# A decoder's gated delta mixer: rows of decay and beta reach all partitions by GpSimd DMAs out of a DRAM scratch, where matmuls with a constant and ScalarE copies did it

## What is computed

```python
qkv, z, a, b = split(h @ w_in)
qkv = silu(causal_conv(qkv))                     # q, k, v of 8 heads
q, k = l2norm(q) * 128 ** -0.5, l2norm(k)
beta = sigmoid(b)                                # (time, 8 heads)
g = -exp(A_log) * softplus(a + dt_bias)          # (time, 8 heads)
G = cumsum(g within a chunk)
S_t = exp(g_t) (I - beta_t k_t k_t^T) S_{t-1} + beta_t k_t v_t^T;   o_t = S_t^T q_t
```

## Time and profile before

| | |
|---|---|
| time, median of 3 runs | 1976.42 us (1971.94 to 1976.88) |
| the profiled execution's own time | 1976.46 us |
| its span, first to last instruction | 1974.7 us |
| busy: PE, PEld, DVE, ACT, POOL | 92%, 87%, 57%, 33%, 0% |
| mean granted TensorE clock | 0.937 of full speed |
| DMA packets | 136.00 MB, mean 69 GB/s |

### The profile page before, as it was taken

One profiled execution on the slowest core, in us unless ns is written; L12 is line 12 of the kernel. 1 busy time (PEld: TensorE's weight loads), 2 busy tenths in 40 slices (PEclk: granted clock), 3 DMA queues, 4 the chain that ended last, 5 costly groups with the idle time before them and its releaser, 6 DMA issues. The chain is left out here.

```text
span 1974.7 us, 33936 instructions
## 1 busy us (share of the span) xinstructions
PE 1811.3 (92%) x13227; PEld 1714.2 (87%) x13227; DVE 1134.3 (57%) x2027; ACT 661.5 (33%) x1108; POOL 0.4 (0%) x5
## 2 busy tenths in 40 slices
PE   3899899998999999997799999999988999999997
PEld 3888888887999989997688888888867999999996
DVE  5777878785534334354666677667732643434344
ACT  1434444432212222222444455445522221222222
POOL 0000000000000000000000000000000000000000
PEclk9988989898999999998799999999957999999997
DMA  5122222222333323222112211211110333322321
GB/s 174 46 64 65 67 63 66 64 66 67 86 94 88 86 76 86 77 77 54 45 44 57 58 37 50 56 56 33 56 34 22 88 89 90 90 86 85 88 82 45
DMA packets 257436, 136.00 MB, mean 69 GB/s; under 512 B 6698, under 2 KB 255876, under 8 KB 257348
## 3 DMA queue, kind: packets, MB, share of 16 engines
q1 hardware_dynamic: 219700, 114.03, 20.4%
q10 hardware_dynamic: 37648, 20.68, 3.5%
HBM read 122.70 MB, written 12.00 MB: 68 GB/s over the span
## 5 line engine op out<-in xcount | busy, mean ns | idle before, releaser
L425 PE MATMUL pj<-xh,w_hi 128*128 128x272 f32 x2064 | 467.2, 309 | 29.8 <-DVE w_lo L1304 15.0
L425 PE MATMUL pj<-xl,w_hi 128*128 128x272 f32 x2064 | 440.4, 296 | 0.0
L425 PE MATMUL pj<-xh,w_lo 128*128 128x272 f32 x2064 | 439.4, 295 | 0.0
L865 ACT ACTIVATE w_hi<-w_raw 128x1024 fp32r<-128x1024 f32 x209 | 220.8, 1056 | 642.3 <-PE pj L425 623.9
L425 PEld LDWEIGHTS pj<-xh,w_hi 128*128 128x128 f32 x2064 | 335.6, 196 | 54.3 <-issue 26.8
L425 PEld LDWEIGHTS pj<-xl,w_hi 128*128 128x128 f32 x2064 | 338.5, 197 | 0.0
L425 PEld LDWEIGHTS pj<-xh,w_lo 128*128 128x128 f32 x2064 | 336.8, 197 | 0.0
L1304 DVE TENSOR_TENSOR w_lo<-w_raw,w_hi 128x1024 fp32r<-128x1024 f32 x209 | 254.8, 1219 | 45.9 <-ACT w_hi L865 45.7
L425 PE MATMUL pj<-oh,w_hi 128*128 128x272 f32 x1280 | 269.0, 292 | 12.7 <-DVE ol L1347 5.4
L425 PE MATMUL pj<-oh,w_lo 128*128 128x272 f32 x1280 | 266.0, 289 | 0.0
L425 PE MATMUL pj<-ol,w_hi 128*128 128x272 f32 x1280 | 266.0, 289 | 0.0
(11 more groups left out here) (275 smaller groups left out, 2050.8 us busy)
## 6 DMA issues: line engine op xcount, KB each, us to landing
w_raw<-in_mlp_w_up_dram SPq DMA_DIRECT2D x64, 512.0 KB, 3.9
w_raw<-in_mlp_w_down_dram SPq DMA_DIRECT2D x64, 512.0 KB, 3.7
w_raw<-in_hgrn_w_in_dram SPq DMA_DIRECT2D x32, 512.0 KB, 4.0
w_raw<-in_gdn_w_in_dram SPq DMA_DIRECT2D x32, 512.0 KB, 4.1
out_dram<-S ACTq DMA_DIRECT2D x16, 512.0 KB, 3.5
S<-in_state_hgrn_dram ACTq DMA_DIRECT2D x8, 512.0 KB, 4.0
w_raw<-in_hgrn_w_out_dram SPq DMA_DIRECT2D x8, 512.0 KB, 3.6
S<-in_state_gdn_dram ACTq DMA_DIRECT2D x8, 512.0 KB, 4.0
```

The source lines that it names most:

```text
L425: last = mm(pj[:, s, b, 0:HALF], w[:, s, k, :], v[:, k, b * HALF:(b + 1) * HALF], start=(k == 0 and a == 0), stop=(k == KT - 1 and a == 2))
L865: f(w_hi[:, c % SPLIT], w_raw[:, slot], ACT.Copy).then_inc(w_high, 1)
```

## The change

The constants for the indicator products and the head's column leave the constant tile, which shrinks from 1264 to 1000 columns. VectorE's select, PE's two products per head, ScalarE's two copies and its exp are gone, with the waits that guarded their PSUM banks. POOL waits for step `eg`, stores the three groups of eight rows of `gt4` into a DRAM tensor (3, 8, 544), waits for all three stores, and then loads for every head one row of each group onto 128 partitions: G as soon as step `qn` of the head before is done, beta and eG as soon as step `cols2` of the head before is done. VectorE waits for the loads at the three places where the tiles are read.

```diff
+            s = st["gp"][1]
+            pool.wait_ge(s.sem, s.after("eg", 0))
+            for n, r in enumerate((0, 32, 96)):
+                pool.dma_start(gates[n], gt4[r:r + H]).then_inc(gates_kept, 16)
+            pool.wait_ge(gates_kept, 48)
+            v = st["ga"][0]
+            for h in range(H):
+                if h:
+                    pool.wait_ge(v.sem, v.after("qn", h - 1))
+                pool.dma_start(gd["G"], gates[0, h].partition_broadcast(P)).then_inc(g_in, 16)
+                if h:
+                    pool.wait_ge(v.sem, v.after("cols2", h - 1))
+                pool.dma_start(gd["beta"], gates[1, h].partition_broadcast(P)).then_inc(beta_in, 16)
+                pool.dma_start(gd["eG"], gates[2, h].partition_broadcast(P)).then_inc(eg_in, 16)
...
-                if slot in ("L3", "L4"):
-                    g, name = (0, "gb") if slot == "L3" else (1, "bb")
-                    pe.wait_ge(s.sem, s.after("G" if g else "hist", h))
-                    pe.wait_ge(v.sem, v.after("gsel", h))
-                    for b in range(2):
-                        last = mm(rr[:, 2 + b, 0:HALF], cf[:, C_IND + g * P:C_IND + (g + 1) * P],
-                                  work[:, b * HALF:(b + 1) * HALF], start=True, stop=True)
-                    t.did(last, name)
...
-                        held((v, "sr3", h), *([] if nxt is None else [(sa, "G", nxt)]))
+                        held((v, "sr3", h))
...
-                        held((s, "rs", h), *([] if nxt is None else [(sa, "bb", nxt)]))
+                        held((s, "rs", h))
...
-                    sem_of(t, "gb", h)
-                    s.did(f(halves(G), rr[:, 2:4, 0:HALF], ACT.Copy), "G")
...
-                    sem_of(t, "bb", h)
-                    s.did(f(halves(gd["beta"]), rr[:, 2:4, 0:HALF], ACT.Copy), "bb")
...
-                    s.did(f(gd["eG"], G, ACT.Exp), "eG")
...
-                    v.did(ts(work, gt4[:], hc[:, 4:5], None, ALU.mult), "gsel")
...
-                    after(s, "G", h)
+                    after(v, "cols", h)
+                    dve.wait_ge(g_in, h * 16 + 16)
...
+                    dve.wait_ge(beta_in, h * 16 + 16)
                     v.did(tt(work, nK, gd["beta"], ALU.mult), "kb")
...
+                    dve.wait_ge(eg_in, h * 16 + 16)
                     v.did(tt(gd["qe"], nQ, gd["eG"], ALU.mult), "qe")
```

More of the change, by code:

```diff
@@ L42 @@
 V_N = V_CONV
-C_EYE, C_INCL, C_NSTR, C_IND, C_RESET, C_SEQ, C_INCLS, C_NSTRS, C_HSEL = 0, 128, 256, 384, 640, 1184, 1192, 1224, 1256
-C_W = C_HSEL + H
+C_EYE, C_INCL, C_NSTR, C_RESET, C_SEQ, C_INCLS, C_NSTRS = 0, 128, 256, 384, 928, 936, 968
+C_W = C_NSTRS + TS
 CU_HALF = len(LEVELS) * (T // 2)
@@ L70, in shape_constants @@
     cf[:, C_NSTR:C_NSTR + P] = -(p[None, :] > p[:, None]).astype(np.float32)
-    cf[0:32, C_IND:C_IND + P] = 1
-    cf[32:64, C_IND + P:C_IND + 2 * P] = 1
     t = np.arange(T)
@@ L80, in shape_constants @@
     cf[:TS, C_NSTRS:C_NSTRS + TS] = -(same & (s[None, :] > s[:, None])).astype(np.float32)
-    cf[:, C_HSEL:C_HSEL + H] = p[:, None] % 32 == np.arange(H)[None, :]
     cu = np.zeros((P, 2, len(LEVELS), T // 2), np.float32)
@@ L235, in build @@
             gp=["x", "neg", "ls", "g", "g2", "scan", "dl"],
-            ga=["cols", "gsel", "k1", "k2", "k3", "kneg", "kls", "q1", "q2", "q3", "qneg", "dec", "ks", "qls",
+            ga=["cols", "k1", "k2", "k3", "kneg", "kls", "q1", "q2", "q3", "qneg", "dec", "ks", "qls",
                 "v1", "v2", "v3", "vneg", "kn", "kb", "qs", "kkd", "vls", "vs", "qn", "zneg", "qkd", "nl", "tt0", "tt1",
@@ L251, in build @@
             gp=["A", "exp", "ln", "be", "el", "eg", "cols"],
-            ga=["hist", "past", "ktap", "qtap", "vhist", "kexp", "kln", "G", "ksig", "qexp", "qln", "bb", "dec",
-                "sqk", "vtap", "qsig", "lnk", "rnk", "eG", "sqq", "vexp", "vln", "vsig", "lnq", "rnq", "zexp", "zln", "cout",
+            ga=["hist", "past", "ktap", "qtap", "vhist", "kexp", "kln", "ksig", "qexp", "qln", "dec",
+                "sqk", "vtap", "qsig", "lnk", "rnk", "sqq", "vexp", "vln", "vsig", "lnq", "rnq", "zexp", "zln", "cout",
                 "K", "tm0", "zsig"],
@@ L265, in build @@
             gp=["cols"],
-            ga=["cin", "gb", "bb", "ssk", "kk", "ssq", "qk", "stash", "t0"],
+            ga=["cin", "ssk", "kk", "ssq", "qk", "stash", "t0"],
             gr=["x2", "dt2", "tr2", "vT", "x4", "dt4", "tr4", "kT", "x8", "sks", "dt8", "tr8", "x16", "dt16", "tr16",
@@ L274, in build @@
         ones_set = sem("ones_set")
+        gates_kept = sem("gate_rows_kept")
+        g_in = sem("decay_rows_spread")
+        beta_in = sem("beta_rows_spread")
+        eg_in = sem("decay_factors_spread")
+        gates = nc.dram_tensor("gate_rows", (3, H, T), F32, kind="Internal").ap()
         st = {}
@@ L683, in gdn_rec @@
                         gdn_prepare("L1", nxt)
-                    if m == 32 and nxt is not None:
-                        held((s, "rs", h))
-                        gdn_prepare("L4", nxt)
                     if m == 64 and nxt is not None:
@@ L1076, in gdn_prepare @@
                     norm_scale(work, "lnk", "rnk", h)
-                    s.did(f(gd["eG"], G, ACT.Exp), "eG")
                 if slot == "L6x":
-                    sem_of(s, "eG", h)
                     sem_of(v, "qs", h)
@@ L1584, in gdn_prepare @@
                 if slot == "L1":
-                    cp(hc[:, 4:5], cf[:, ds(h + C_HSEL, 1)])
                     cp(hcw[:], cw[:].rearrange("p j (g x) -> p j g x", g=3)[:, :, :, ds(h, 1)]
@@ L1588, in gdn_prepare @@
                     v.did(cp(gnext[:], of_head(0).rearrange("p c o -> p (c o)")), "cols")
-                    after(v, "cols", h)
-                    v.did(ts(work, gt4[:], hc[:, 4:5], None, ALU.mult), "gsel")
                     low(h * 4, U_GIN + 3)
```

## The result

The changed kernel takes 1985.89 us (median of 7 runs, 1980.38 to 1990.41), the kernel before, run beside it, 1974.25 us (7 runs, 1970.39 to 1977.94). The ratio is 1.0058, with a 95% interval of 1.0041 to 1.0075: slower by 11.6 us, where 1972.4 and no measurable difference had been forecast, and the time lies above the range.

The account below looks back on a forecast made before the run. PE, busy 1811.3 of 1974.7 us, was taken to set the pace. 3.29 + 0.35 + 0.51 + 0.32 - 0.40 = 4.07 us off 1976.46 gave 1972.4 us, counted as the same; range 1963 to 1981.

Parts of the forecast that it names:

- The sum: Whole kernel: beta's product 3.29, G's product 0.35, head 0 0.51, constants 0.32, less waits 0.40, gives 4.07 us gained.
- the four rivals: Alternatives: all PE time returns (0.20), waits eat the gain (0.08), POOL's DMAs hold VectorE (0.10), clock falls (0.06).
- rival 4: Recurrences: PE's clock falls to half in more stretches; 1996 us with two more each, 1984 with one; chance 0.06.
- the mixer's terms: Second mixer: 3.29 for beta's product, 0.35 for G's, 0.51 for head 0, less 0.40 us for waits.
- G's product: In seven recurrences: removing it leaves PE waiting for Tt's copy, so only 0.05 us each, 0.35 us in all.
- beta's product: In seven recurrences: without it VectorE's merge (L1719) starts 0.47 us earlier, behind `w_lo`; 3.29 us in all.
- rival 1: All PE time of the 64 removed records, 15.4 us, comes back; 1960.7 us; chance 0.20.
- The start: Kernel start: the constant tile shrinks by 132 KB, so everything waiting for constants begins 0.32 us earlier.
- Head 0: Head 0's preparation, with no recurrence to hide it: 0.51 us of ScalarE's chain go.
- The loads: GpSimd's loads of 272 KB take 2.2 to 4.1 us each by size, all hidden.
- Rival 3: Head's end and `qn`: 21 POOL DMAs hold VectorE up, 1991 us at 0.9 us each; decides from 0.48; chance 0.10.
- The eight waits ahead of `kb`: VectorE's wait for the loads between the norm of k and the next product: 8 x 0.05 = 0.40 us lost.

Follow-up runs that it names:

- before_clear: The kernel before with 40 idle instructions (satisfied waits) at the start of TensorE's program, so that neither MLP loop has gaps; 1961.37 us (6 runs).
- after_clear: The changed kernel with 40 idle instructions (satisfied waits) at the start of TensorE's program, so that neither MLP loop has gaps; 1957.71 us (6 runs).
- the doubled loads: The changed kernel with the 40 idle instructions, GpSimd issuing every load a second time into a scratch in DRAM; 1959.26 us (7 runs).

## Why the prediction was wrong, point by point

**What failed.** The step is a term that "The sum" does not have. It adds up 3.29 + 0.35 + 0.51 + 0.32 - 0.40 for the second mixer and the start, and puts everything else, the second MLP too, at nothing without a reason. Removing 75 instructions from PE's program moves all code behind them, and the second MLP's loop moved from place 3 to 184, onto the 41 places at which its jumps back stall. That is +15.04 us, more than three times the sum. None of the four rivals was it: rival 4 had the sign, by another mechanism, the clock in the recurrences; that its 1984 us lies near the measured time is luck. The trace of before had the sign of it: two MLPs with the same code, 344.55 and 329.87 us, and in the first one's loop, right at the jump back,

```profile
698.07 0.49 PE L425 MATMUL pj<-xh,w_hi 128*128 128x272 f32 x2 [2.83 <-DVE w_lo L1304]
...
701.03 0.61 PE L425 MATMUL pj<-xh,w_hi 128*128 128x272 f32 x2 [1.97 <-issue]
```

I had read the mixer's rows and the start alone.

**The terms of the sum.** Together the mixer's terms held; the split between them did not quite. The places of the earlier trace rows in after's recurrence:

```profile
1139.36 0.58 ACT L1157 ACTIVATE ws<-rr 128x512 f32<-128x512 f32 x1
...
1140.00 1.10 PE L684 MATMUL rr<-ws 128*128 128x64 f32 x8 [0.79 <-ACT ws L1157]
...
1144.81 0.60 ACT L1157 ACTIVATE ws<-rr 128x512 f32<-128x512 f32 x1 [2.72 <-PE rr L480]
...
1148.29 1.21 DVE L1304 TENSOR_TENSOR w_lo<-w_raw,w_hi 128x1024 fp32r<-128x1024 f32 x1
...
1149.43 0.44 DVE L1719 COPY_PREDICATED ws<-cu,rr 128x256 f32<-128x256 uint8 x1
```

Where G's product stood, PE now waits 0.79 us for the copy of Tt and starts right behind it, as forecast. But the 0.05 us put down for it did not come: from this copy to level 16's it is 1147.85 - 1142.41 = 5.44 us before and 1144.81 - 1139.36 = 5.45 after. The merge (L1719) stands behind `w_lo` without its 0.47 us of idle time, and from level 16's copy to it the way falls from 1153.02 - 1147.85 = 5.17 to 1149.43 - 1144.81 = 4.62. So the whole gain is at beta's product: 0.55 for 0.47. A recurrence without any half clock, before and after:

```profile
1129.67:1194.93 65.26, 61.01 (x451) 54.14 (x451) 45.32 (x103) 31.93 (x70) 0.00 (x0) 1.00 0.19 50
```

```profile
1126.64:1191.25 64.61, 59.66 (x443) 52.80 (x444) 44.66 (x100) 30.27 (x68) 1.60 (x3) 1.00 0.24 64
```

is 0.65 us shorter, for 0.52 in the sum; over six, at equal half clock (13.7 us in before_clear and after_clear), it is 395.08 against 391.96, 0.52 each. PE's busy time falls by 1.35 in one recurrence, and half of it comes back as waiting, which is why rival 1 (all of PE's time) fell.

**The start.** PE's first product starts at 15.43 us instead of 16.02, 0.59 for the 0.32 of the sum. Whether it arrives can't be told: the first MLP begins 0.74 us later in the profiled pair, and over all traces at 509.14 to 511.30 in the kernel before and its versions and at 506.79 to 511.45 in the changed one's.

**Head 0.** From `eg` (L996 before, L1002 after) to the sum of squares of k it is 956.29 - 919.09 = 37.20 us before and 954.40 - 917.70 = 36.70 after: -0.50, for -0.51. PE waits longer for it now, as ScalarE's part of the chain is what is left:

```profile
954.40 2.18 PE L463 MATMUL rr<-ws,ones 128*128 128x272 f32 x4 [4.37 <-ACT ws L1072]
```

**The loads.** GpSimd's issues (busy us, mean ns, idle before) and their landing:

```profile
L420 POOL DMA_DIRECT2D ws<-gate_rows x8 | 4.3, 541 | 334.8 <-DVE ws L1625 333.3 <-DMA gate_rows<-gt 1.6
...
ws<-gate_rows POOLq DMA_DIRECT2D x24, 272.0 KB, 4.0
...
gate_rows<-gt POOLq DMA_DIRECT2D x3, 17.0 KB, 1.8
```

4.0 us for 272 KB is the upper end of the 2.2 to 4.1 that I gave, and nothing waits for it. Rival 3 is excluded, at the 0.48 us for each load that it needed, by the doubled loads, and with it, at that size, the collision on the ports that the Trainium skill's page "SBUF — State Buffer" ("Who interferes with whom") let one fear: VectorE is busy for 44.66 us in a recurrence, 0.66 less than before, at three POOL instructions in each. The eight waits ahead of `kb` (0.40) could not be told apart from nothing.

**The clock.** Of rival 4 a small part is there. Its reading of the earlier trace rows was not right: the products of 4 columns (L693) run at 1069.87 to 1071.77, ahead of the 3.4 us at half clock, and what PE does in these is tiles of a projection and a level's product. At half clock in the six recurrences, the six traces of the kernel before and its shifted versions have 13.7 or 17.1 us; the changed kernel's six have 13.7 to 34.1 (23.9 in the profiled one). Two runs of the same shifted kernel show what that costs, 13.7 us and 30.7 us:

```profile
981.93:1373.89 391.96, 363.41 (x2653) 322.61 (x2654) 266.50 (x592) 181.42 (x402) 9.60 (x18) 0.98 0.24 64
```

```profile
978.85:1377.50 398.65, 370.16 (x2653) 329.29 (x2653) 266.43 (x592) 181.61 (x401) 9.63 (x18) 0.96 0.24 63
```

6.7 us for 17 us more at half clock: more than the whole gain. So in some executions the clock takes the gain of the recurrences back. Whether the change calls these stretches forth (PE waits 0.79 us at a new place) or they fall so by chance stays open; the doubled loads, with 6.8 us, had the fewest, which speaks against the transfers as their cause.

## What to carry to other kernels

Before a prediction counts an edit's stages, compare the passes of each loop with one another: if two passes, or two copies of the same code, differ in length with PE idle at the jump back, the loop may lie badly in the program, and any edit ahead of it that changes the number of instructions on that engine can move it in or out. Such a shift has its own term in the sum, and it is cheap to win: forty idle instructions where PE waits anyway are worth 14.7 us in the traces of the kernel before and 27.5 in those of the changed one (by the medians some 16 and 28), more than the change itself could bring. To judge an edit, measure it with the loops out of the way on both sides.

## What had not been expected of the hardware

A loop of 1578 instructions on PE, 99 KB, costs nothing at its jump back or 4.3 to 8.1 us, by its place in the program alone; at 195 it does, at 198 it doesn't. The half clock that follows is part of the price: at place 184 the PE gaps are 9.4 us (PE busy for 335.51 of 344.91), and PE's busy time is 5.64 us longer than the 329.87 of the undisturbed loop. And an idle instruction on PE, a satisfied wait, took 0.103 us, so 177 of them are 18 us where nothing hides them.
